# Which activation tables ScalarE loads, and where, in a two-block network (hybrid attention layers and a mixture of experts) on one core

## The chip, the core and the metric

The kernel runs on one core of a Trainium2 chip. The core has five engines with a program of their own each: TensorE (PE in the profile, its weight loads PEld), VectorE (DVE), ScalarE (ACT), GpSimd (POOL) and SyncE (SP), which here only issues DMA transfers. They wait for one another through semaphores. ScalarE evaluates functions such as Exp, Ln and Sigmoid from a table set that has to be loaded before; a load is an instruction of its own, ACT_TABLE_LOAD, on ScalarE's queue. The metric is the device time of one execution in microseconds (us); three executions of the kernel before gave 2309.46, 2310.67 and 2312.57 us.

## The reference, cut to what matters

Everything is float32, one sequence of 256 tokens, width 1024. First come two layers, each a gated delta rule (8 heads) beside a differential attention (8 heads), then one layer of a second block with a mixture of 32 experts, 4 per token.

```
def first_block(x, ...):
    for l in range(2):
        h = rmsnorm(x, norm_w[l])
        proj = h @ w_in[l]
        q_a, k_a, v_a, ab_a, z_a, q_b, k_b, v_b, z_b, gate_a, gate_b = split(proj)
        y_a = gated_delta_branch(q_a, k_a, v_a, ab_a, z_a, ...)
        y_b = diff_attention_branch(q_b, k_b, v_b, z_b, ...)
        merged = sigmoid(gate_a) * (y_a @ w_pa[l]) + sigmoid(gate_b) * (y_b @ w_pb[l])
        x = x + merged @ w_out[l]
    return rmsnorm(x, final_norm_w)

def gated_delta_branch(q, k, v, ab, z, ...):
    qkv = silu(short_conv(concat(q, k, v), conv_w))        # Sigmoid table
    q = l2norm(q); k = l2norm(k)                           # rsqrt as Exp(-0.5 * Ln)
    beta = sigmoid(ab[:2]); g = -exp(a_log) * softplus(ab[2:] + dt_bias)
    o = chunk_gated_delta(forward) + chunk_gated_delta(backward)   # exp of decays
    return rmsnorm(o, norm_w) * silu(z)

def diff_attention_branch(q, k, v, z, ...):
    a = softmax(q0 k0) - lam * softmax(q1 k1)
    return rmsnorm(a @ v, subln_w) * (1 - lambda_init) * silu(z)

def second_block(x, ...):
    h = rmsnorm(x, g_mix); z = h @ w_in
    x = x + concat(pool_mixer(u), dilated_attention(q, k, v)) @ w_out
    x = x + moe(rmsnorm(x, g_ffn), ...)                    # 32 experts, 4 per token
    x = x + (p @ w_ple_proj) * sigmoid(rmsnorm(x, g_ple) @ w_ple_gate)
    return rmsnorm(x, g_final)

def expert_block(xb, e):
    g, u = split(xb @ w_gate_up[e] + b_gate_up[e])
    g = min(g, 7); u = clip(u, -7, 7)
    return ((u + 1) * g * sigmoid(1.702 * g)) @ w_down[e] + b_down[e]
```

## The kernel before

Each engine has its own function, written in the order in which it works; the semaphores between them are set by hand, and nothing reorders the instructions. The loops over layers (l) and heads (n) are unrolled, and the expert loop is a real loop of 32 turns. The one thing that the author of the kernel does not write is most of the table loads: the build puts an ACT_TABLE_LOAD ahead of an activation when the set that it takes for active lacks the function. A call of `preload_act_table_set` puts a load where it stands and names the set that is active from there on. The set "natural_log_exp_and_others" holds both Ln and Exp; the kernel before asks for it at L1041, ahead of the first layer, and at L1319, behind the expert loop. Copy and Square never have a load in front of them.

The stages of a layer, with the names that the text below uses:

- Norm at the layer's start. ScalarE squares and sums the rows of x (L1044), then `ss_rstd` makes 1/sqrt by Ln (L1025) and Exp (L1026); VectorE scales (L1363), TensorE turns the result (`transpose16`, L519). The norm behind the last layer, the norm ahead of the second block and the one ahead of the router use the same `ss_rstd` (their squares are L1020).
- Convolution. TensorE makes the projections (`product`, L527), ScalarE copies them (L1091), VectorE convolves, ScalarE applies Sigmoid to each of 12 units (L1069).
- Segment stage. TensorE makes twelve more products u = 0 to 11 of 16 instructions each (L527). Behind the products u = 0, 1, 2 and 4 it makes two column sums each (`norm_sums`, L578) for the norms of q and k; a sum i waits for ScalarE's square i (`unit_squares`, L1075). Behind the products u = 3, 5, 7 and 9 come two Gram products each (`gram`, L587 and L588), on which VectorE waits (`gram_decay`, L1515). ScalarE, in order: copy of product u (L1106), then for the two sums behind it `unit_rnorms` (Ln at L1081, Exp at L1083) and the square of the unit two further on. The square that TensorE waits for behind product u = 1 thus stands behind the Ln and Exp of the unit two before it. VectorE inverts 16x16 blocks (`invert_base`, L1547 and L1551), four heads at a time, once behind the Gram products of the heads 0 to 3 and once for the heads 4 to 7; head 0 of the head loop cannot get far before the second has ended.
- Head loop, 8 heads. TensorE works at head n and at the rest of head n-1. ScalarE for head n-1: attention_squares (L1148), attention_rstd (Ln L1153, Exp L1154), the z gate in three steps (Exp L1171, Ln L1175, Exp L1179), chunk_rstd (Ln L1142, Exp L1143); for head n the softmax (Exp L1165). The result of L1154 lets VectorE finish head n-1's attention (`attention_y`, L1655), and this frees the bank into which TensorE writes the scores of head n (L663).
- Merge. ScalarE makes the gates' sigmoids from Exp, Ln and Exp (L1219, L1222, L1225), TensorE multiplies (L754, L527), VectorE combines (L1749, L1751).

In the second block there are eight small products for a bias table (L803) behind the last layer, a dilated attention, the router and the expert loop: per turn 64 TensorE instructions for gate and up (L948), 32 for down (L971), one Sigmoid on ScalarE (L1313), and 12.6 MB of weights which SyncE asks for as slots come free. TensorE starts a turn with eight bias products (L939), for which the bias rows, last in the turn's transfers, must have landed.

Of the kernel before, what the change touches and what calls it, by code (L numbers as in the profile page):

```python
# [110 lines left out]
def block_kernel(nc, a, out):  # L111
    ctx = ExitStack()
    with ctx:
# [5 lines left out]
        def s(name):  # L119

            if name not in sems:
                sems[name] = ctx.enter_context(nc.semaphore(name))
            return sems[name]
# [875 lines left out]
        def _(act):  # L999
# [48 lines left out]
            for l in range(DEPTH):  # L1048
# [16 lines left out]
                def sigmoid_unit(u):  # L1065
                    act.wait_ge(s("conv_sb"), l * 12 + u + 1)
                    if u >= 2:
                        act.wait_ge(s("silu_sb"), l * 12 + u - 1)
                    act.activation(sgm[u % 2], conv_o[u % 2], ACT.Sigmoid).then_inc(s("sgm_sb"), 1)  # L1069

                def unit_squares(i):
                    act.wait_ge(s("silu_sb"), l * 12 + NORM_UNITS[i] + 1)
                    if i >= 2:
                        act.wait_ge(s("qk_norm_ps"), l * 8 + i - 1)
                    act.activation(qk_sq[i % 2].rearrange("p (b c) -> p b c", b=2), qkv_unit(NORM_UNITS[i]), ACT.Square).then_inc(s("qk_sq"), 1)  # L1075
# [18 lines left out]
                unit_squares(0)  # L1094
                unit_squares(1)
                sigmoid_unit(11)

                act.wait_ge(s("gcum_cp"), l + 1)
                act.activation(eg[:, :], gcum[:, :], ACT.Exp)
# [198 lines left out]
            def gathered(n):  # L1298
                act.wait_ge(s("gather_ps"), n)
                act.activation(Xs, pb[3][:, :], ACT.Copy).then_inc(s("X_sb"), 1)  # L1300

            def turned(n):
                act.wait_ge(s("XT_ps"), n)
                act.activation(XT, pb[3][:, :].rearrange("p (c h t) -> p c h t", c=4, h=2), ACT.Copy).then_inc(s("XT_sb"), 1)

            gathered(1)
            turned(1)
            act.wait_ge(s("rounds_known"), 1)
# [669 lines left out]
```

## Time and profile before

| | |
|---|---|
| three executions | 2309.46, 2310.67 (median), 2312.57 us |
| profiled execution | 2312.8 us, of which the span from the first to the last instruction is 2311.0 us |
| TensorE busy | 2128.1 us, 92% of the span |
| VectorE busy | 743.6 us, 32% |
| ScalarE busy | 674.7 us, 29% |
| GpSimd busy | 104.8 us, 5% |
| granted TensorE clock, mean | 0.941 of full speed |
| DMA | 551.08 MB, mean 238 GB/s |

How to read it: times are microseconds from the span's start unless marked ns. A timeline row has its start, its busy time, engine, line, operation, output and inputs, how many instructions it merges, and in brackets the idle time of the engine before it and what ended it. TensorE's instructions overlap: a following one starts while the last is in its tail. In the rows by stretch the numbers are the stretch's length, then the busy time (and instructions) of PE, PEld, DVE, ACT and POOL, the granted clock (1.00 is 2.4 GHz, 0.50 is 1.2 GHz), the share of the DMA engines that was busy, and GB/s. In the groups by line, the busy total and the mean in ns of one instruction stand behind the bar, then the idle time ahead of them.

### The profile page before, as it was taken

How to read it: one execution, taken by the hardware profiler on the slowest of the kernel's cores; microseconds unless marked ns; L12 is line 12 of the kernel's file. 1: busy time of each engine (PE TensorE's matmuls, PEld its weight loads, DVE VectorE, ACT ScalarE, POOL GpSimd, SP SyncE). 2: the span in 40 equal slices, each digit the busy share in tenths (PEclk: the TensorE clock that was granted, in tenths of full speed). 3: DMA queues.
4: the chain of work that ended last, by engine and by line, in shares of the span. 5: the costliest groups of instructions: out<-in, count | busy, mean ns of one | idle time of the engine just before them, and what ended most of it. 6: DMA issues, size and time to landing. Idle time of an engine off the chain costs nothing.

```text
span 2311.0 us, 23579 instructions
## 1 busy us (share of the span) xinstructions
PE 2128.1 (92%) x9025; PEld 1095.7 (47%) x9025; DVE 743.6 (32%) x2024; ACT 674.7 (29%) x1210; POOL 104.8 (5%) x84
## 2 busy tenths in 40 slices
PE   4989999998989999999977899999999999999997
PEld 4844777444854677544454433333333333333333
DVE  2657566211565766411131211111111111111112
ACT  2162588421244388721221111111111111111112
POOL 0030111000012121000000000000000000000000
PEclk9999899997999999999877799999999999999998
DMA  5633211343443221345531499999999999999980
GB/s 169 230 117 118 73 37 47 137 145 109 174 154 109 73 74 37 110 145 181 184 155 59 193 427 426 424 428 410 427 415 427 416 428 414 425 428 423 412 358 19
DMA packets 102324, 551.08 MB, mean 238 GB/s; under 512 B 8789, under 2 KB 13041, under 8 KB 77170
## 3 DMA queue, kind: packets, MB, share of 16 engines
q1 hardware_dynamic: 102258, 550.21, 59.4%
q8 instruction: 40, 0.66, 0.1%
q14 instruction: 26, 0.21, 0.0%
HBM read 546.98 MB, written 3.21 MB: 238 GB/s over the span
## 4 chain that ended last, share of the span: by engine, by line
PE 48%; DMA 10%; DVE 4%; ACT 3%; issue 1%; SPq 1%; DVEq 0%
PE bank L948 20%; DMA region<-b_gate_up_dram 10%; PE bank L527 10%; PE bank L971 4%; PE bank L754 2%; PE bank L939 2%; PE bank L921 1%; PE bank L907 1%; PE bank L616 1%; PE bank L519 1%; SPq L389 1%; PE bank L628 0%; PE bank L663 0%; DVE region L1646 0%; PE bank L643 0%
## 5 line engine op out<-in xcount | busy, mean ns | idle before, releaser
L948 PE MATMUL bank<-ring,region 128*64 128x512 f32 x2048 | 474.3, 623 | 0.0
L948 PEld LDWEIGHTS bank<-ring,region 128*64 128x64 f32 x2048 | 150.0, 144 | 326.0 <-issue 326.0
L1889 DVE TENSOR_SCALAR region<-bank 128x512 f32<-128x512 f32 x32 | 22.1, 691 | 755.6 <-PE bank L948 755.6
L527 PE MATMUL bank<-ring,hT 128*128 128x512 f32 x576 | 257.7, 605 | 2.2 <-issue 1.2
L527 PE MATMUL bank<-ring,region 128*128 128x512 f32 x432 | 193.1, 606 | 4.8 <-ACT region L1012 1.8
L527 PEld LDWEIGHTS bank<-ring,hT 128*128 128x128 f32 x576 | 111.4, 195 | 140.3 <-issue 138.8
L527 PE MATMUL bank<-hT,ring 128*128 128x256 f32 x768 | 171.9, 387 | 0.0
L1313 ACT ACTIVATE region<-region 128x512 f32<-128x512 f32 x32 | 20.2, 630 | 519.4 <-DVE region L1889 519.4
L527 PEld LDWEIGHTS bank<-hT,ring 128*128 128x128 f32 x768 | 149.1, 195 | 21.2
L527 PEld LDWEIGHTS bank<-ring,region 128*128 128x128 f32 x432 | 83.7, 195 | 110.6 <-issue 106.8
L971 PE MATMUL bank<-ring,region 128*64 128x512 f32 x512 | 116.9, 597 | 11.3 <-issue 11.3
L616 PE MATMUL bank<-ring,hT 128*128 128x512 f32 x256 | 125.6, 603 | 0.0
L971 PE MATMUL bank<-region 128*64 128x512 f32 x512 | 116.2, 592 | 0.0
L754 PE MATMUL bank<-ring,hT 128*128 128x512 f32 x256 | 111.5, 592 | 0.0
L1317 ACT ACTIVATE region<-bank 128x512 f32<-128x512 f32 x32 | 19.1, 597 | 219.0 <-PE bank L971 219.0
L939 PE MATMUL bank<-region,ones 1*64 1x512 f32 x256 | 38.8, 677 | 46.0 <-DMA region<-b_gate_up_dram 33.9
L1953 POOL TENSOR_TENSOR region<-ring,c_main_sb 128x512 f32<-128x512 f32 x48 | 62.9, 1315 | 353.1 <-PE bank L628 305.2
L1447 DVE SCALAR_TENSOR_TENSOR region<-region,conv_wT 128x256 f32<-128x256 f32 x192 | 78.0, 478 | 0.0
L971 PEld LDWEIGHTS bank<-region 128*64 128x64 f32 x512 | 44.2, 137 | 65.6 <-issue 65.6
L754 PEld LDWEIGHTS bank<-ring,hT 128*128 128x128 f32 x256 | 48.0, 190 | 57.4 <-issue 57.4
L971 PEld LDWEIGHTS bank<-ring,region 128*64 128x64 f32 x512 | 40.4, 136 | 65.7 <-issue 65.7
L921 PE MATMUL bank<-region 64*128 64x512 f32 x264 | 65.8, 615 | 0.7 <-ACT region L1317 0.7
(337 smaller groups left out, 2487.5 us busy)
## 6 DMA issues: line engine op xcount, KB each, us to landing
ring<-w_gate_up_dram SPq DMA_DIRECT2D x128, 2048.0 KB, 11.2
ring<-w_in_dram SPq DMA_DIRECT2D x44, 2048.0 KB, 7.9
ring<-w_down_dram SPq DMA_DIRECT2D x32, 2048.0 KB, 9.9
region<-w_down_dram SPq DMA_DIRECT2D x32, 2048.0 KB, 11.4
ring<-w_out_dram SPq DMA_DIRECT2D x5, 2048.0 KB, 8.1
ring<-rows_scratch SPq DMA_DIRECT2D x4, 2048.0 KB, 9.2
ring<-w_pa_dram SPq DMA_DIRECT2D x4, 2048.0 KB, 8.0
ring<-w_pb_dram SPq DMA_DIRECT2D x4, 2048.0 KB, 8.3
```

The lines of the kernel that those rows point to most:

```text
L389: sp.dma_start(dst, src, **kw).then_inc(s(name), 16)
L519: last = pe.transpose(pb[kp][:, (2 * kk + t) * P:(2 * kk + t + 1) * P], src(t, 2 * kp + kk), ident)
L527: mm = pe.matmul(dst, lhs(k), w(k), start=(k == 0), stop=(k == n_k - 1))
L616: mm = pe.matmul(pb[3][:, :], hT[:, k, t * P:(t + 1) * P], w[:, k, :], start=(k == 0), stop=(k == KC - 1))
L754: mm = pe.matmul(pb[GATE_BANKS[kind][t]][:, :], hT[:, k, t * P:(t + 1) * P], w[:, k, :], start=(k == 0), stop=(k == KC - 1))
L907: mm = pe.matmul(pb[3][hf * 64:(hf + 1) * 64, :], P1[:, t, :], h2[:, t, hf * NB:(hf + 1) * NB], start=(t == 0), stop=(t == 1))
L921: mm = pe.matmul(pb[4 + 2 * t + hf][:, :], CT[hf * 64:(hf + 1) * 64, t, :], ysb[hf * 64:(hf + 1) * 64, :], start=False, stop=False, skip_g ...
L939: pe.matmul(pb[g][hf * 64:(hf + 1) * 64, :], ones[32 * g:32 * g + 1, 0:64], bpad[32 * g:32 * g + 1, hf * NB:(hf + 1) * NB], start=True, st ...
L948: mm = pe.matmul(pb[g][hf * 64:(hf + 1) * 64, :], XT[:, 2 * (j % 2) + kk, j // 2, :], wj[:, kk, c:c + NB], start=False, stop=(j == 3 and k ...
L971: mm = pe.matmul(pb[2][hf * 64:(hf + 1) * 64, :], actT[:, c, j, :], wj[:, c, hf * NB:(hf + 1) * NB], start=(j == 0 and c == 0), stop=(j == ...
L1447: ins = dve.scalar_tensor_tensor(dst, src, w, dst, ALU.mult, ALU.add)
L1953: pool.tensor_tensor(Lv[q].rearrange("p (d t) c -> p d t c", d=2), LT_all[:, n].rearrange("p (d t) c -> p d t c", d=2), lvl[:, q].unsqueez ...
```

## The change

Two lines are added to ScalarE's program. In each layer, behind the last Sigmoid of the convolution, the set with Ln and Exp is asked for by name; ahead of the expert loop, before ScalarE waits for the first gathered tokens, the set with Sigmoid is asked for.

```
                 unit_squares(0)
                 unit_squares(1)
                 sigmoid_unit(11)
+                act.preload_act_table_set("natural_log_exp_and_others")
 
                 act.wait_ge(s("gcum_cp"), l + 1)
                 act.activation(eg[:, :], gcum[:, :], ACT.Exp)
...
                 act.activation(XT, pb[3][:, :].rearrange("p (c h t) -> p c h t", c=4, h=2), ACT.Copy).then_inc(s("XT_sb"), 1)
 
+            act.preload_act_table_set("sigmoid_and_others")
             gathered(1)
             turned(1)
             act.wait_ge(s("rounds_known"), 1)
```

From the first line on, every line number is one higher, and from the second on, two.

ScalarE in the segment stage, kernel before, the copy of product u = 0 and what follows it up to the second square (L1106 is the copy, L1081 and L1083 are Ln and Exp, L1075 is the square):

```order
L1106 ACTIVATE region<-bank 128x512
L1081 ACT_TABLE_LOAD
L1081 ACTIVATE region<-bank,small 128x512
L1083 ACT_TABLE_LOAD
L1083 ACTIVATE region<-region 128x512
L1075 ACTIVATE region<-region 128x512
L1081 ACT_TABLE_LOAD
L1081 ACTIVATE region<-bank,small 128x512
L1083 ACT_TABLE_LOAD
L1083 ACTIVATE region<-region 128x512
L1075 ACTIVATE region<-region 128x512
```

The same place in the changed kernel:

```order
L1107 ACTIVATE region<-bank 128x512
L1081 ACTIVATE region<-bank,small 128x512
L1083 ACTIVATE region<-region 128x512
L1075 ACTIVATE region<-region 128x512
L1081 ACTIVATE region<-bank,small 128x512
L1083 ACTIVATE region<-region 128x512
L1075 ACTIVATE region<-region 128x512
```

The four loads are gone and the order of the rest is kept.

ScalarE in the head loop, kernel before, from the copy ahead of the scores (L1158) to the softmax (L1165) of a head n above 0:

```order
L1158 ACTIVATE region<-bank 128x512
L1153 ACT_TABLE_LOAD
L1153 ACTIVATE small<-small 128x2
L1154 ACT_TABLE_LOAD
L1154 ACTIVATE small<-small 128x2
L1171 ACTIVATE region<-region 128x512
L1119 ACTIVATE region<-bank 128x512
L1134 ACTIVATE region<-bank,eg 128x128 x2
L1175 ACT_TABLE_LOAD
L1175 ACTIVATE region<-region,small 128x512
L1165 ACT_TABLE_LOAD
L1165 ACTIVATE region,small<-bank,small 128x256 x4
```

The same place in the changed kernel:

```order
L1159 ACTIVATE region<-bank 128x512
L1154 ACTIVATE small<-small 128x2
L1155 ACTIVATE small<-small 128x2
L1172 ACTIVATE region<-region 128x512
L1120 ACTIVATE region<-bank 128x512
L1135 ACTIVATE region<-bank,eg 128x128 x2
L1176 ACTIVATE region<-region,small 128x512
L1166 ACTIVATE region,small<-bank,small 128x256 x4
```

Here too four loads are gone; two more go further on in the same head, at L1142 and L1143.

ScalarE around the expert loop in the changed kernel, from the last copy of the router on (L1315 is the Sigmoid in the loop):

```order
L1298 ACTIVATE region<-bank 32x256
L1307 ACT_TABLE_LOAD
L1301 ACTIVATE region<-bank 128x512
L1305 ACTIVATE region<-bank 128x512
L1311 TENSOR_LOAD rounds_i
L1311 ISA x2
L1313 UNCONDITIONAL_BRANCH
L1313 ISA
L1315 ACTIVATE region<-region 128x512
```

In the kernel before the load stood inside the loop, ahead of the Sigmoid; it now stands once, ahead of the loop. In the whole program of the changed kernel nine table loads are left: L1032, L1039 and L1041 at the start, L1069 and L1097 in each layer, L1307, and L1321 behind the expert loop. The other engines' programs are as they were.

## Rows read from the trace of the kernel before

**Rows 1.** Busy time by stretch: up to the expert loop, and the expert loop.

```profile
0.00:1299.00 1299.00, 1188.70 (x4759) 754.45 (x4759) 580.32 (x1684) 538.84 (x1018) 104.75 (x84) 0.93 0.33 119
1299.00:2253.00 954.00, 896.83 (x4160) 321.11 (x4160) 147.23 (x316) 118.55 (x161) 0.00 (x0) 0.97 0.98 415
```

**Rows 2.** Groups of ScalarE by line: table loads, and the loop's Sigmoid.

```profile
L1313 ACT ACT_TABLE_LOAD x32 | 41.1, 1283 | 0.8 <-issue 0.3
L1313 ACT ACTIVATE region<-region 128x512 f32<-128x512 f32 x32 | 20.2, 630 | 519.4 <-DVE region L1889 519.4
...
L1319 ACT ACT_TABLE_LOAD x1 | 1.3, 1283 | 0.0
```

**Rows 3.** Timeline of PE, segment stage of the second layer.

```profile
669.82 7.03 PE L527 MATMUL bank<-ring,hT 128*128 128x512 f32 x16
681.47 1.72 PE L578 MATMUL bank<-region,ones 128*128 128x512 f32 x2 [4.62 <-ACT region L1075]
685.93 2.07 PE L578 MATMUL bank<-region,ones 128*128 128x512 f32 x2 [2.74 <-ACT region L1075]
687.80 9.18 PE L527 MATMUL bank<-ring,hT 128*128 128x512 f32 x16
...
778.03 2.05 PE L628 MATMUL bank<-region 128*128 128x128 f32 x8 [3.78 <-DVE region L1624]
```

**Rows 4.** Timeline of PE, the same place of the first layer.

```profile
151.18 7.84 PE L527 MATMUL bank<-ring,hT 128*128 128x512 f32 x16
```

**Rows 5.** Timeline of ACT, segment stage of the second layer.

```profile
676.97 1.28 ACT L1081 ACT_TABLE_LOAD   x1
678.27 0.69 ACT L1081 ACTIVATE region<-bank,small 128x512 f32<-128x512 f32 x1
...
680.80 0.61 ACT L1075 ACTIVATE region<-region 128x512 f32<-128x512 f32 x1
```

**Rows 6.** Timeline of DVE, segment stage of the second layer.

```profile
706.56 0.69 DVE L1515 TENSOR_TENSOR ring<-ring,bank 128x512 f32<-128x512 f32 x1 [11.07 <-PE bank L588]
```

**Rows 7.** Timeline of PE, end of the first layer's merge.

```profile
493.74 27.63 PE L527 MATMUL bank<-ring,region 128*128 128x512 f32 x64
523.48 2.41 PE L519 MATMUL bank<-c_main_sb,region 128*128 128x128 f32 x16 [2.10 <-DVE region L1751]
526.78 30.14 PE L527 MATMUL bank<-ring,region 128*128 128x512 f32 x64 [0.89 <-issue]
```

**Rows 8.** Busy time by stretch, within the row at 526.78.

```profile
525.00:531.00 6.00, 5.11 (x10) 2.33 (x9) 1.12 (x4) 0.66 (x2) 0.00 (x0) 0.50 0.01 3
```

**Rows 9.** Chain of waits, one head of the second layer (start, us, what).

```profile
841.87 1.28 ACT L1154
...
844.16 1.14 PE bank L663 x8
```

**Rows 10.** Timeline of PE, the instructions ahead of that wait.

```profile
842.95 1.05 PE L628 MATMUL bank<-region 128*128 128x128 f32 x8
```

**Rows 11.** Waits of PE up to 1300 (total, times, longest).

```profile
PE bank L663 <- DVE region L1655: 1.5, 10, 0.2
```

**Rows 12.** Timeline of ACT, norm at the second layer's start.

```profile
558.84 1.28 ACT L1025 ACT_TABLE_LOAD   x1
```

**Rows 13.** Timeline of PE, the three places behind such norms.

```profile
563.61 3.65 PE L519 MATMUL bank<-c_main_sb,region 128*128 128x128 f32 x16 [6.70 <-DVE region L1363]
...
1092.89 12.09 PE L803 MATMUL bank<-region,rel 33*128 33x512 f32 x16 [0.78 <-DVE x L1767]
1106.67 3.68 PE L519 MATMUL bank<-c_main_sb,region 128*128 128x128 f32 x16 [1.70 <-DVE region L1363]
...
1267.26 3.67 PE L519 MATMUL bank<-c_main_sb,region 128*128 128x128 f32 x16 [7.71 <-DVE region L1365]
```

**Rows 14.** Chain of waits, two turns of the expert loop.

```profile
1686.78 16.60 PE bank L948 x64
...
1717.75 13.91 PE bank L948 x64
```

More of the change, by code:

```diff
@@ L1096, in _ @@
                 sigmoid_unit(11)
+                act.preload_act_table_set("natural_log_exp_and_others")
                 act.wait_ge(s("gcum_cp"), l + 1)
@@ L1304, in turned @@
                 act.activation(XT, pb[3][:, :].rearrange("p (c h t) -> p c h t", c=4, h=2), ACT.Copy).then_inc(s("XT_sb"), 1)
+            act.preload_act_table_set("sigmoid_and_others")
             gathered(1)
```

## The prediction

> **What bounds the kernel now.** I read the busy time by stretch first [rows 1]. TensorE is busy for 1188.7 of the first 1299 us and for 897 of the 954 us of the expert loop; in the loop the DMA engines are busy for 0.98 of the time at 415 GB/s, so the loop goes by the transfers, with TensorE close behind. ScalarE is busy for 539 us in the first part and 119 us in the loop: nowhere the bound as a whole. So what its table loads cost can't be had from their sum. It has to be looked for where TensorE stands still and the wait leads back through ScalarE, and in the views of the waits there are few such places: the segment stage of each layer, one wait in each head, and the norms between the stages.
>
> **The loads that go.** The groups of ScalarE by line list 194 loads in 22 groups, from 32 at L1313 to one at L1319, each 1.283 us [rows 2]. Nine are left, so 185 go, 237 us of ScalarE's time. A load takes 1.30 us out of a chain: 676.97 to 678.27 [rows 5], that is 1.28 and a gap of 0.02. The load that now stands behind the last Sigmoid of the convolution is the one that stood one line further on; it costs nothing new.
>
> The Trainium skill (ScalarE: Activation LUTs, section on what ACT_TABLE_LOAD costs) adds a drain of 1380 ns to the 1283 ns of a load, 2.66 us for a switch. The trace doesn't agree: the activation starts 1.30 us behind the load's start, as said. By the page each load below would count twice, and the norms alone would bring some 5 us more; I go by the row.
>
> **Segment stage.** Here is most of the gain. In the second layer TensorE has ended product u = 1 at 681.47 - 4.62 = 676.85, waits 4.62 us for the square of L1075, makes one column sum, waits 2.74 us for the next square, and starts product u = 2 at 687.80 [rows 3]. On ScalarE two loads lie ahead of the first of these squares and four ahead of the second, from 676.97 on without a gap [rows 5]. What releases that chain at 676.97 is VectorE's work on the decays and stays. So the first sum comes 2.60 us earlier, at 678.87, and the second 5.20 us earlier, at 680.73. The two waits shrink to about 2.0 and 1.0 us. TensorE's 16 instructions take 7.03 us at full clock [rows 3], so about 0.86 for the two of a sum: product u = 2 starts at 681.6, 6.2 us earlier.
>
> The clock comes on top. The product at 687.80 took 9.18 us instead of 7.03: 2.15 us lost because the granted clock had fallen in the wait to the lower of its two levels, 1.2 of 2.4 GHz. In the first layer the same product took 7.84 us, 0.81 lost [rows 4]. If the clock now stays up in the shorter waits, the second layer gains 6.2 + 2.15 = 8.4 and the first 6.2 + 0.8 = 7.0, together 15.4 us. If it falls, each layer loses again about what the wait at the end of the merge costs: 2.10 us of waiting, then a product of 64 instructions in 30.14 instead of 27.63 us, 2.5 us lost at a clock of 0.50 [rows 7, 8]. Then the two gain 15.4 - 5.0 = 10.4. The wait of 2.10 us is just as long as the one that stays here, so the fall is likelier; I take 12 us, 6 for each layer. Ends: nothing (a rival below) and 15.4.
>
> Does it last? What follows is driven by TensorE: VectorE waited 11.07 us for the Gram product at 706.56 [rows 6], and it then works almost without a pause until it releases head 0's next step at 778.03, for which TensorE had waited 3.78 us [rows 3]. VectorE's chain begins with that Gram product, so it moves with TensorE, and so does the start of the head loop. ScalarE has slack behind it: the squares for the later sums are ready before their product ends already now. The weights' transfers run at 119 GB/s against 415 in the loop [rows 1], so they keep up.
>
> **Head loop.** A head takes some 20.6 us, and TensorE has hardly a gap in it. The chain passes through the loads of L1153 and L1154 and VectorE's L1655 to the scores at 844.16 [rows 9]. But the instructions ahead of the scores start at 842.95 and are busy for 1.05 us, up to 844.00 [rows 10]: of the 2.60 us that leave this chain TensorE can use 0.15, which is the wait that the profile lists, 1.5 us in ten heads [rows 11]. There are 14 such heads: 14 x 0.15 = 2.1 us. Ends: nothing, and 14 x 0.32 = 4.5 us if the scores could start as tightly as other products do (0.16 us ahead of their predecessor's end). The other four loads of a head lie under TensorE's work: the softmax comes 2 us earlier, but VectorE, which needs it, is at that time still busy with the keys, and the step behind it waits for VectorE. ScalarE falls from nearly full in a head to some three fifths; nobody there waits for it any more.
>
> **Norms.** `ss_rstd` has two loads in four of its six calls, 2.60 us each call [rows 12]. At the second layer's start and ahead of the router TensorE waits for the norm alone, 6.70 and 7.71 us [rows 13]: 2.6 us each, 5.2. The clock is down at both places, and waits of 4.1 and 5.1 us leave it down. The two calls behind the last layer follow one another, 5.2 us in all, but TensorE makes the bias table's products beside them: those run from 1092.89 for 12.09 us, to 1104.98, and the next work started at 1106.67 [rows 13]. So 1.7 us can be had, and 3.5 are hidden. Together 6.9 us; ends 5.2 and 8.
>
> **Merge, gates, expert loop.** The merge's 16 loads lie beside products of 27 us, for which VectorE waits anyway: nothing. In the expert loop the load ran right behind the turn's last copy, with 0.8 us of idle time before all 32, and the Sigmoid then waited 519.4 us for VectorE [rows 2]: removing 41.1 us of loads there brings nothing. The load added ahead of the loop lies in ScalarE's wait for the first gathered tokens, which is longer than 10 us: nothing; 1.3 us if that cover were gone. Behind it only the copies of the first tokens are queued. The loop as a whole starts earlier by the whole gain, since its transfers start when TensorE frees the first slot; the first expert's weights have landed well before.
>
> **Sum.** 12 + 2.1 + 6.9 = 21.0 us. The profiled execution took 2312.8 us, so 2291.8; it stood 2.1 us above the median of 2310.67, which gives 2289.7 us.
>
> **Rivals.**
> The clock stays up. The waits of 2.0 and 1.0 us leave the granted clock at its upper level in both layers, and the heads give their upper end: 15.4 + 4.5 + 6.9 = 26.8 us, 2283.9 us. For it: at the waits of now the clock was lost for only 0.81 us in one of the layers. Against: the fall behind a wait of 2.10 us [rows 7].
>
> The segment stage gives its gain back. Product u = 2 starts earlier, but VectorE or the decays become the bound ahead of the head loop, so that only heads and norms are left: 9.0 us, 2301.7 us. For it: TensorE already waits 3.78 us for VectorE there. Against: VectorE's own idle 11.07 us, which say that it is TensorE that feeds it.
>
> Nothing happens. Either the loads weren't in anyone's way, or the expert loop's transfers, the real bound, don't start earlier: 2310.7 us. Against: the transfers of the loop wait for slots that TensorE frees. A rule of the Trainium skill would have it so as well: by the page ScalarE activation tables: per-element evaluation and per-set limits, section on table sets in the compiler and the runtime, the loads are placed by the longest run that one set serves, and then Ln beside Exp would have shared a set already. The trace of before doesn't agree: each Ln and each Exp of L1081 and L1083 has its own load.
>
> Slower. The expert loop sits at the edge between transfers and TensorE's clock: a turn whose gate and up products meet the lower clock has them in 16.60 instead of 13.91 us, and takes 1717.75 - 1686.78 = 31.0 us [rows 14] against a mean of 954 / 32 = 29.8 [rows 1]. If the earlier start put all turns into that state, they would cost 32 x 1.2 = 38 us: 2289.7 + 38 = 2328 us. It decides from 18 such turns on. Against: a turn that long lets the transfers get ahead, the wait at its start goes, and with it the reason for the fall.
>
> **Chances.** The forecast 0.63 (its own range 2286 to 2294), the clock staying up 0.15, the gain given back 0.13, nothing 0.04, slower 0.05. The range, 2281 to 2301 us, holds the first two and half of the third. A change of less than 0.2%, 4.6 us, can't be told from none here: faster by more 0.92, the same 0.03, slower 0.05.
>
> **What would show it.** The profile after should have 9 table loads and ScalarE busy for about 437 us. In both layers the two waits of L578 should be near 2.0 and 1.0 us, VectorE's first wait for a Gram product some 2 us longer than 11.07 (it is fed sooner by ScalarE than by TensorE), and the wait of 3.78 us ahead of head 0 unchanged. The wait for L1655 ahead of the scores should be gone, with heads of 20.4 us. The norm waits should read 4.1 and 5.1 us, and the one behind the bias table none. The expert loop should take 954 us as before. It is wrong if the head loop starts no earlier against the layer's start, if another engine's wait grows there by what L578 loses, or if the loop's length moves by more than 3 us.

## The result, and the profile after

The changed kernel takes 2274.82 us (median; 2273.50 to 2275.65), beside 2310.07 us of the kernel before on the same chip: a ratio of 0.9844 with a 95% interval of 0.9831 to 0.9856, or 35 us less. The forecast was 2289.7 us, 21 us less, and 2281 to 2301 as a range. The direction was right, and the time lies outside the range: two fifths of the gain weren't foreseen.

The profiled execution took 2274.37 us, its span is 2272.6 us, the mean granted clock 0.956 (before 0.941). The busy time of the engines, from the profile page:

```profile
PE 2108.8 (93%) x9025; PEld 1086.3 (48%) x9025; DVE 739.3 (33%) x2024; ACT 435.7 (19%) x1025; POOL 104.8 (5%) x84
```

ScalarE is busy for 435.7 us, where 437 was expected. TensorE is busy for 19.3 us less than before, although its 9025 instructions are the same ones. What differs is the granted clock, and for the clock the forecast had some 3 us at most (2.15 and 0.8 in the two segment stages): the first sign of what it left out. Busy time by stretch, up to the expert loop and in the loop (columns as in [rows 1]):

```profile
0.00:1261.70 1261.70, 1169.29 (x4757) 745.13 (x4757) 576.12 (x1684) 340.88 (x865) 104.77 (x84) 0.95 0.34 122
1261.70:2216.20 954.50, 898.62 (x4160) 321.64 (x4160) 147.15 (x316) 77.50 (x129) 0.00 (x0) 0.96 0.98 414
```

The loop is as long as it was, 954.5 against 954.0 us; the 37.3 us that are gone by its start were gained ahead of it. Timeline of TensorE in the segment stage of the second layer, beside [rows 3]:

```profile
665.21 1.12 PE L578 MATMUL bank<-region,ones 128*128 128x512 f32 x2 [1.92 <-ACT region L1075]
666.97 1.13 PE L578 MATMUL bank<-region,ones 128*128 128x512 f32 x2 [0.63 <-ACT region L1075]
667.93 7.03 PE L527 MATMUL bank<-ring,hT 128*128 128x512 f32 x16
...
756.01 2.05 PE L628 MATMUL bank<-region 128*128 128x128 f32 x8 [3.77 <-DVE region L1626]
```

The waits of 4.62 and 2.74 us are 1.92 and 0.63 now, and the clock stayed up: the product takes its full-clock 7.03 us, where it took 9.18. VectorE still waits for the first Gram product, 11.37 against 11.07 us [rows 6], and the wait of 3.77 us ahead of head 0 is what it was, so the gain goes on into the head loop:

```profile
684.54 0.69 DVE L1517 TENSOR_TENSOR ring<-ring,bank 128x512 f32<-128x512 f32 x1 [11.37 <-PE bank L588]
```

The chain of waits in one head of the second layer (start, us, what), beside [rows 9], no longer passes through ScalarE:

```profile
818.27 0.89 PE bank L628 x8
819.16 1.07 PE bank L663 x8
```

And TensorE at the first layer's end, at the second layer's start, behind the last layer and ahead of the router, beside [rows 7, 13]:

```profile
515.14 1.97 PE L519 MATMUL bank<-c_main_sb,region 128*128 128x128 f32 x16 [2.10 <-DVE region L1753]
518.00 27.70 PE L527 MATMUL bank<-ring,region 128*128 128x512 f32 x64 [0.90 <-ACT region L1012]
549.84 3.65 PE L519 MATMUL bank<-c_main_sb,region 128*128 128x128 f32 x16 [4.14 <-DVE region L1365]
...
1077.44 3.67 PE L519 MATMUL bank<-c_main_sb,region 128*128 128x128 f32 x16
...
1232.19 3.39 PE L519 MATMUL bank<-c_main_sb,region 128*128 128x128 f32 x16 [5.15 <-DVE region L1367]
1236.47 5.10 PE L527 MATMUL bank<-region,hT 128*128 128x32 f32 x32 [0.89 <-ACT hT L1012]
```

The norms' waits fell by 2.56 us each, 6.70 to 4.14 and 7.71 to 5.15, and the 1.70 us behind the bias table are gone. But look at what stands next to them. At the first layer's end TensorE waits the same 2.10 us as before, and the product of 64 instructions takes 27.70 us where it took 30.14 [rows 7]. In the router, 32 instructions take 5.10 us. The kernel before has them in 7.01:

```profile
1271.83 7.01 PE L527 MATMUL bank<-region,hT 128*128 128x32 f32 x32 [0.89 <-issue]
```

No load went from the first of these places. In the router none stood between these instructions either, but the wait ahead of them had lost two; experiments 2 and 5 have the same instructions behind a wait that is not shortened.

**The ledger.** Since TensorE's instructions are the same in both kernels, the start of each can be compared one by one. Of the stages' lengths I took the mean over four profiled executions on each side (the kernel before with e2, e5 and e6 of the experiments below, the kernel after with e1, e7 and e8: they differ from these two only in the loop's loads, or by one or two loads ahead of the first norm):

| | gained, us | forecast |
|---|---|---|
| segment stage, first and second layer | 7.3 and 7.9 | 12 for both |
| heads | 3.1 in 14 heads | 2.1 |
| norms | 2.56, 2.1 and 2.56 | 6.9 |
| granted clock, where no load left | 9.4 | none |
| start (first transfers), expert loop, end | 1.2 early, then 2.4 lost | 0 |
| sum | 33.7 | 21.0 |

The 9.4 us are 1.8 in the first layer's last products, 1.2 in the two first heads, 1.7 in the second layer's last products, 1.4 in the second block's z products, 1.0 between those and the router and 2.3 from the router to the gathering. The row of the start and the loop scatters by as much between executions of one kernel. So do two parts of the 9.4: the first heads (88 instructions behind TensorE's wait of 3.78 us took 16.1 to 19.6 us in the executions before, 16.1 to 18.9 after) and the first layer's last products, where one of the four executions before, e6, lost no more than the kernel after.

### The profile page after: what moved, and what is told of

Its sections match the earlier page's. It is cut to its first block, busy times and chain, and to the rows that moved or that the text cites. A ratio compares the mean times of both kernels' runs of the same rounds, so it can differ in the third digit from the quotient of the medians.

```text
span 2272.6 us, 23394 instructions
## 1 busy us (share of the span) xinstructions
PE 2108.8 (93%) x9025; PEld 1086.3 (48%) x9025; DVE 739.3 (33%) x2024; ACT 435.7 (19%) x1025; POOL 104.8 (5%) x84
## 4 chain that ended last, share of the span: by engine, by line
PE 51%; DMA 10%; DVE 4%; ACT 1%; issue 1%; SPq 1%; DVEq 0%
PE bank L948 21%; PE bank L527 10%; DMA region<-b_gate_up_dram 10%; PE bank L971 5%; PE bank L754 2%; PE bank L939 2%; PE bank L616 1%; PE bank L921 1%; PE bank L907 1%; PE bank L628 1%; SPq L389 1%; PE bank L639 1%; PE bank L519 1%; PE bank L803 1%; DVE region L1648 0%
## 5 line engine op out<-in xcount | busy, mean ns | idle before, releaser
L527 PE MATMUL bank<-ring,hT 128*128 128x512 f32 x576 | 251.1, 592 | 2.2 <-issue 1.2
L527 PE MATMUL bank<-ring,region 128*128 128x512 f32 x432 | 189.4, 597 | 4.8 <-ACT region L1012 3.6
L527 PEld LDWEIGHTS bank<-ring,hT 128*128 128x128 f32 x576 | 108.7, 190 | 135.1 <-issue 133.6
L527 PE MATMUL bank<-hT,ring 128*128 128x256 f32 x768 | 171.5, 386 | 0.0
L527 PEld LDWEIGHTS bank<-hT,ring 128*128 128x128 f32 x768 | 148.7, 194 | 21.0
L527 PEld LDWEIGHTS bank<-ring,region 128*128 128x128 f32 x432 | 82.3, 192 | 107.9 <-issue 101.9
L1315 ACT ACTIVATE region<-region 128x512 f32<-128x512 f32 x32 | 20.2, 630 | 561.8 <-DVE region L1891 561.8
L616 PE MATMUL bank<-ring,hT 128*128 128x512 f32 x256 | 125.0, 601 | 0.0
L971 PE MATMUL bank<-region 128*64 128x512 f32 x512 | 116.2, 592 | 0.0
L754 PE MATMUL bank<-ring,hT 128*128 128x512 f32 x256 | 111.5, 592 | 0.0
L907 PE MATMUL bank<-region 128*64 128x512 f32 x264 | 63.7, 604 | 0.0
```

Of the source, the lines that this page charges most:

```text
L527: mm = pe.matmul(dst, lhs(k), w(k), start=(k == 0), stop=(k == n_k - 1))
L616: mm = pe.matmul(pb[3][:, :], hT[:, k, t * P:(t + 1) * P], w[:, k, :], start=(k == 0), stop=(k == KC - 1))
L754: mm = pe.matmul(pb[GATE_BANKS[kind][t]][:, :], hT[:, k, t * P:(t + 1) * P], w[:, k, :], start=(k == 0), stop=(k == KC - 1))
L907: mm = pe.matmul(pb[3][hf * 64:(hf + 1) * 64, :], P1[:, t, :], h2[:, t, hf * NB:(hf + 1) * NB], start=(t == 0), stop=(t == 1))
L971: mm = pe.matmul(pb[2][hf * 64:(hf + 1) * 64, :], actT[:, c, j, :], wj[:, c, hf * NB:(hf + 1) * NB], start=(j == 0 and c == 0), stop=(j == ...
```

## Experiments

**1. Which of the two calls.** Kernel after without the call ahead of the loop, and kernel before with that call alone.

```
-            act.preload_act_table_set("sigmoid_and_others")     # e1: from after
+            act.preload_act_table_set("sigmoid_and_others")     # e2: into before
             gathered(1)
```

> The change without the second call: Ln and Exp share a set in the layers, the Sigmoid's load stays inside the expert loop (32 loads). Theory (the loop's loads lie in ScalarE's wait and cost nothing): the same as the changed kernel, 2274.8 us, within 1.5 us. Rival (the loop's loads are worth something, for example 0.3 us a turn, which would explain part of the 14 us that the forecast missed): 2284 us or more, and a longer expert loop than 954 us.

Measured: 2276.62 us (2274.18 to 2279.37), ratio to the kernel before 0.9851 [0.9835, 0.9866].

> The second call alone: 32 loads leave the expert loop, all of the layers' loads stay. Theory: the same as before, 2310.1 us within 1.5 us, the expert loop at 954 us. Rival (loop loads cost): 2300 us or less.

Measured: 2310.43 us (2305.08 to 2317.12), ratio 1.0006 [0.9994, 1.0018]. The gain comes from the call in the layer: e1 is far from its rival's 2284 us, though 1.8 us above the changed kernel, where the theory allowed 1.5. The 32 loads of the loop stood in an idle time of 519 us [rows 2] and were worth nothing that these runs show, as forecast. Over the profiles of this document the loop took 953.5 to 957.7 us with them and 952.0 to 956.6 without, so a us would not be seen.

**2. The segment stage alone, and all but it.** From the kernel after: the loads return behind product u = 9 by asking for another set there, or the call is made only there.

```
                 for u in range(12):
                     act.wait_ge(s("seg_ps"), l * 12 + u + 1)
+                    if u == 9:      # e3, with the call of after kept
+                        act.preload_act_table_set("exp_and_others")
+                    if u == 9:      # e4, in place of the call of after
+                        act.preload_act_table_set("natural_log_exp_and_others")
```

> The set with Ln and Exp serves only from the convolution's end to segment product 9; behind that another set with Exp alone is asked for, and the loads of heads, merge and norms come back as before. Theory (the segment stage's waits and their clock are 7.1 and 8.2 us by the comparison of the two traces): 2310.1 - 15.4 = 2294.7 us, the waits of L578 at 2.0 and 1.0 us, the clock up behind them in both layers. Second theory (an earlier start also moves later stages against the falls of the clock): up to 10 us less than that, 2285 us. Rival (the forecast's 12 us): 2298 us.

Measured: 2285.80 us (2283.65 to 2289.55), ratio 0.9897 [0.9877, 0.9917]: 24.9 us less than before, where the second theory had put it.

> The loads of the segment stage stay (16 Ln and 16 Exp in the two layers), all others leave. Theory by waits alone: heads 3.1 us and norms 7 us by the comparison of the traces, 2300 us. Second theory (the rest of the gain, 23 us of span, belongs to these stages and to the clock behind them): 2287 us. Between the two would show that part of the clock's gain hangs on where the segment stage ends, not on the loads that left.

Measured: 2295.00 us (2292.61 to 2295.43), ratio 0.9931 [0.9916, 0.9947]: 15.7 us less, between the two theories' 2300 and 2287 us. The two gains make 40.6 us, more than the 34 to 35 of both together, so part of each is one that either of them brings. In e3 the segment stages are 15.7 us shorter than in the profiled execution before. The other 9 lie elsewhere, where e3 has the same loads as the kernel before. The plainest place is the router (timeline of TensorE, e3), behind the unshortened wait of 7.71 us for the norm:

```profile
1245.76 3.68 PE L519 MATMUL bank<-c_main_sb,region 128*128 128x128 f32 x16 [7.71 <-DVE region L1369]
1250.33 4.49 PE L527 MATMUL bank<-region,hT 128*128 128x32 f32 x32 [0.90 <-issue]
```

The same wait, the same 32 instructions, and 4.49 in place of 7.01 us. The length of the wait just ahead does not decide what the clock costs.

**3. The program as a whole later.** If it were the absolute time at which a wait falls, a delay far ahead would shift all of it. One or two loads more (1.3 us each) ahead of the first norm, in the kernel before (e5, e6) and after (e7, e8).

```
                 in_layer.fence()
+                if l == 0:
+                    for name in NAMES:      # one name, or two
+                        act.preload_act_table_set(name)
                 ss_rstd(in_layer)
```

> The kernel before with one table load more (1.3 us) ahead of the first norm, on the path of everything: all that follows is 1.3 us later and otherwise as it was. Theory A (the gain that the waits don't explain comes from where in time the waits fall against the clock's own rhythm, and that is fixed to the program's start): the time moves by something other than 1.3 us, by 3 us or more either way, so not within 2310.5 to 2313.5. Theory B (the clock falls by chance from execution to execution, and its mean loss depends on the waits alone): 2312.0 us, within 1.5.

Measured: 2312.40 us, ratio 1.0013 [1.0004, 1.0022].

> The kernel before with two table loads more (2.6 us) ahead of the first norm. Theory A: off the straight line by 3 us or more here or in the run with one load. Theory B: 2313.3 us within 1.5.

Measured: 2311.45 us, ratio 1.0010 [1.0001, 1.0019].

> The changed kernel with one table load more (1.3 us) ahead of the first norm. Theory A: off 2276.5 us by 3 us or more, up to 2285, since a favourable place is lost. Theory B: 2276.5 us within 1.5.

Measured: 2276.62 us, ratio 0.9851 [0.9836, 0.9867].

> The changed kernel with two table loads more (2.6 us) ahead of the first norm. Theory A: off 2277.8 us by 3 us or more here or in the run with one load. Theory B: 2277.8 us within 1.5.

Measured: 2277.74 us, ratio 0.9869 [0.9854, 0.9884]. The medians moved by 2.4 and 1.5 us in the kernel before and by 1.8 and 2.9 us in the kernel after (beside the 2274.82 us measured on another chip), for 1.3 and 2.6 us added. None is off by the 3 us that theory A asked for; e6 is 1.9 us below theory B's figure, which allowed 1.5. In the profiles the early stages scatter: the 64 instructions of [rows 7] took 27.70 us in e6, the kernel before with two more loads:

```profile
529.16 27.70 PE L527 MATMUL bank<-ring,region 128*128 128x512 f32 x64 [0.89 <-ACT region L1012]
```

But late stages came out alike however late the program had started: from the router to the gathering 21.62 us in e5 and e6 beside 21.63 before, 19.69 and 19.74 us in e7 and e8 beside 19.72 after.

From this I formed a second theory: what the clock costs at a wait is set by how much work lies between it and the last fall of the clock. By this theory a fall takes up the shift that the program brings along, behind it the program stands against the falls of the clock as it does in every execution of the same kernel, and a change of the work in between, as the one studied here, moves all later falls. One run already at hand fits only in part: e1, whose program is the kernel after's up to the loop, took 18.93 us in that stage and not 19.7.

**4. More work, no other wait.** The theory's test: the kernel before with r more product instructions (0.86 us each; the trace counts each as two) at the start of the second layer's merge. Their result is overwritten, and no load or wait is changed.

```
+                if l == 1:
+                    w = w_wait(l, 16)
+                    for _ in range(r):      # 1, 2, 3
+                        pe.matmul(pb[GATE_BANKS[0][0]][:, :], hT[:, 0, 0:P], w[:, 0, :], start=True, stop=True)
                 gate_part(0, 0, 0, range(0, 4))
```

> The kernel before with one more product instruction (about 0.86 us of TensorE's work, its result overwritten) at the start of the second layer's merge; no table load is changed. Theory A (where a wait falls against the clock's rhythm decides what the clock costs there, and that goes by the amount of work since the clock's last fall): the stages behind it change their lengths although nothing in them is changed: the output product at the second layer's end (28.49 us to the bias products before, against 28.48 in the changed kernel; 4.15 us ahead of it against 2.86), the z products of the second block (62.85 against 60.87) or the stage from the router to the gathering (21.62 against 18.9 to 19.7), by 0.5 us or more in at least one; the time is off 2310.9 by a us or more in one of the three kernels with more work. Theory B (the clock's loss hangs on the length of the waits alone): all later stages keep their lengths to 0.1 us, and the time is 2310.0 + 0.9 = 2310.9 us.

Measured: 2307.92 us (2303.50 to 2310.12), ratio 0.9987 [0.9977, 0.9997].

> As the kernel with one more product instruction there, with two (about 1.7 us). [...] Theory B: later stages as before, 2310.0 + 1.7 = 2311.7 us.

Measured: 2309.86 us, ratio 0.9999 [0.9990, 1.0008].

> As the kernel with one more product instruction there, with three (about 2.6 us). Theory A: again other lengths of the later stages than with one and with two, time anywhere from 2308 to 2315 us, not on one line with the two others. Theory B: later stages as before, 2310.0 + 2.6 = 2312.6 us.

Measured: 2310.40 us, ratio 1.0005 [0.9992, 1.0017]. The kernel before ran at 2310.75 us beside them. Behind the merge TensorE turns 16 tiles and makes the output product. In the kernel before (first row) the turn was in part at the lower level of the clock; with two more instructions (second row, e10) it was at the upper one, as in the kernel after:

```profile
1060.26 3.25 PE L519 MATMUL bank<-c_main_sb,region 128*128 128x128 f32 x16 [2.11 <-DVE region L1751]
```

```profile
1059.42 1.97 PE L519 MATMUL bank<-c_main_sb,region 128*128 128x128 f32 x16 [2.11 <-DVE region L1755]
1062.28 27.70 PE L527 MATMUL bank<-ring,region 128*128 128x512 f32 x64 [0.90 <-ACT region L1016]
```

The wait is 2.11 us in both. One caution: executions of one kernel still differ here. Ahead of the edit they come in groups, told apart by the stage of head 0 of the second layer (from the 3.8 us wait on). In the group of 19.5 us the turn and the product together (L519 to the bias table) took 32.63, 32.65, 32.62 and 32.65 us without added work (before, e2, e6 and e12 below), and 31.35 with two instructions more. In the group of 17.1 us they took 34.22 us twice without (e5, e14), 32.67 with one (e9) and 31.35 with three (e11). Within these two groups each addition shortened what follows, by 1.3 to 2.9 us for 0.9 to 2.6 us of work. But e13 below, the kernel before's program up to here, stood in neither group (19.9 us) and took 31.35 us with nothing added, so this value alone does not show an effect of the added work. The stage from the router on was 21.62 us in all three, as without added work.

**5. The same in the second block,** where 4.7 of the 9.4 us had been gained: r more such instructions ahead of the last z product.

```
+                for _ in range(r if u == 7 else 0):      # 1, 2, 3
+                    pe.matmul(pb[7][:, :], hT[:, 0, P:2 * P], slot_w(slot)[:, 0, :], start=True, stop=True)
                 product(pb[4 + u % 4][:, :], ...
```

> The kernel before with one more product instruction (0.86 us at full clock) ahead of the last z product of the second block; no load is changed. Theory A (position against the clock's falls, set by the work since the last one): one or more of the three stages behind it change by 0.5 us or more: to the first turn for the router (before: 38.36 us with the norm's loads), the router's stage up to the gathering (21.62), and the mixer's (54.67). In the kernel with the segment loads alone removed they read 37.20, 19.12 and 54.64 with the same instructions as before. Theory B: these three stay to 0.1 us, and the time is 2310.5 + 0.9 us.

Measured: 2306.56 us (2303.55 to 2312.81), ratio 0.9984 [0.9974, 0.9995].

> As the one with one more product instruction ahead of the last z product, with two (1.7 us). Theory A: one of the three with more work reads 19.0 to 20.0 us in the stage from the router to the gathering in place of 21.62, so that added work is given back. Theory B: 21.62 in all three, the time 2310.5 + 1.7 us.

Measured: 2308.67 us, ratio 0.9992 [0.9983, 1.0002].

> As the two before, with three (2.6 us). Theory A: the stages behind it differ from those with one and with two by half a us or more, so the time is not on one line with them. Theory B: stages as before, the time 2310.5 + 2.6 us.

Measured: 2308.57 us, ratio 0.9988 [0.9977, 0.9999]. The kernel before: 2309.34 us beside them. Timeline of TensorE, e12, where the kernel before has 7.01 us:

```profile
1268.98 4.19 PE L527 MATMUL bank<-region,hT 128*128 128x32 f32 x32 [0.89 <-issue]
```

The kernel does 0.86 us more work, and its median is 2.8 us lower (by the interval 1.2 to 6.0). From the first z product to the loop it takes 186.39 us with one more, 185.64 with two and 186.44 with three, and 187.62 without. By the rival these would be 188.5, 189.3 and 190.2. So the profiled executions gain 1.2 to 2.0 us by the loop's start. The stage of 19.0 to 20.0 us that was expected of one of the three came with three more (19.40); it is 0.6 us off the one with one more and 0.4 off the one with two, where 0.5 was asked for. The granted clock shows it in the stretch of the 32 instructions (the kernel before, then e12, by stretch):

```profile
1272.00:1279.00 7.00, 6.84 (x32) 6.70 (x32) 0.55 (x3) 0.00 (x0) 0.00 (x0) 0.50 0.58 228
```

```profile
1269.00:1273.20 4.20, 4.17 (x32) 4.04 (x32) 0.64 (x2) 0.00 (x0) 0.00 (x0) 0.87 0.94 372
```

The table puts the executions side by side, in us: from the last turn of the second layer (L519) to the bias table, from the mixer (L826) to the router's turn (2.56 us added where the norm's loads are gone), and from the router (L527) to the gathering (L907). No wait in these stages lost a load but the norm's.

| kernel | L519 to bias table | L826 to router's turn | router to L907 |
|---|---|---|---|
| before, e2, e6 | 32.62 to 32.65 | 93.04 to 93.05 | 21.62 to 21.63 |
| e5 | 34.22 | 93.04 | 21.62 |
| after, e7, e8 | 31.34 to 31.35 | 91.71 to 91.77 | 19.69 to 19.74 |
| e1 | 31.35 | 93.03 | 18.93 |
| e3 | 31.35 | 91.85 | 19.12 |
| e4 | 31.35 | 93.18 | 18.68 |
| e9, e10, e11 | 32.67, 31.35, 31.35 | 93.04 | 21.62 |
| e12, e13, e14 | 32.65, 31.35, 34.22 (ahead of the edit) | 93.04, 92.00, 91.56 | 18.81, 18.99, 19.40 |

The last column settles for the second block that the clock's cost is no property of the waits: seven executions of the kernel before, plain, without the loop's loads, or with loads added at the start or work in the second layer's merge, read 21.62 or 21.63 us, and three with more work just ahead read 18.8 to 19.4. It does not settle the second theory. In e3 the loads and the work are the kernel before's from the second layer's product u = 9 on, the clock fell several times in between, and the stage still reads 19.12; and e1 differs from the kernel after by 0.8 us at the same program. Both stood in the group of e13 at head 0 of the second layer. So what happened some hundreds of us earlier can reach this stage.

**6. The wait that was left.** In both kernels ScalarE's copy of product u = 0, with the Ln, Exp and squares behind it, stands behind four decay exponentials (L1087), which wait for VectorE. The kernel after with these four behind the squares:

```
-                for n in range(4):
-                    decay_exp(n)
                 for u in range(12):
...
                                 unit_squares(i + 2)
+                    if u == 0:
+                        for n in range(4):
+                            decay_exp(n)
                     if u == 1:
```

> The changed kernel with ScalarE's first four decay exponentials of a layer (L1087, which wait for VectorE) moved from ahead of the copy of product u = 0 to behind it and the two squares that follow. The squares for the sums behind product u = 1 are then ready before that product ends. Main theory (these waits were ScalarE's queue behind VectorE's decays): the waits of about 2.0 and 1.0 us in each layer go, the products start 3 us earlier in each layer, and the time is 2274.8 - 6 = 2268.8 us, with up to 3 us more or less by where the clock falls in the later stages. Rival (the Gram products and with them the head loop hang on VectorE's decays, which now come later, or the wait only moves to the sums behind product u = 2): 2273 to 2276 us.

Measured: 2264.51 us (2258.00 to 2265.87), ratio to the kernel before 0.9797 [0.9783, 0.9812], some 10 us faster than the changed kernel and 4.3 us below the expected 2268.8, for which 3 us were allowed. Timeline of TensorE in the second layer: the waits for L1075 are gone.

```profile
647.84 1.02 PE L578 MATMUL bank<-region,ones 128*128 128x512 f32 x2
648.69 7.03 PE L527 MATMUL bank<-ring,hT 128*128 128x512 f32 x16
655.56 1.88 PE L578 MATMUL bank<-region,ones 128*128 128x512 f32 x4
657.28 7.03 PE L527 MATMUL bank<-ring,hT 128*128 128x512 f32 x16
```

The two segment stages became 3.1 and 3.3 us shorter, as expected. Most of the other 4 us came in head 0 of the first layer, which took 18.90 us after and 15.54 here, behind a wait of 3.78 us in both; e1 had 16.12 there with the program of the kernel after. It is the clock again, by stretch (the kernel after, then this one):

```profile
238.00:242.00 4.00, 4.00 (x18) 3.70 (x18) 1.96 (x7) 1.93 (x8) 0.00 (x0) 0.50 0.00 0
```

```profile
234.00:238.00 4.00, 4.00 (x26) 3.04 (x26) 3.58 (x13) 1.93 (x8) 0.00 (x0) 0.99 0.00 0
```

It is the fastest version found.

## Why the prediction was wrong

**What held.** Nothing is won in the merge and the expert loop, and nothing of the segment stage's gain is given back: the rival that VectorE becomes the bound there is out by the 11.37 us of its wait (though the forecast had it grow to some 13 us). The waits of L578 came out at 1.92 and 0.63 us for a forecast of 2.0 and 1.0, the norms at 7.2 us for 6.9. The Trainium skill (ScalarE: Activation LUTs, What ACT_TABLE_LOAD costs) has 2.66 us for a switch, by which estimate two loads cost 5.3 us at a norm. The trace doesn't agree: the two norm waits fell by 2.56 us, so 1.28 us a load was the right price. The rival with nothing happening falls as well.

**Two terms too small.** The segment stage gained 15.2 us, the forecast's upper end (15.4), for which it had 12. The step that failed is "The wait of 2.10 us is just as long as the one that stays here, so the fall is likelier". Behind waits of 1.92 and 0.63 us the clock stayed up in both layers, in all executions with these loads gone. The heads gave 0.22 us each and not 0.15, between the forecast and its end of 0.32: the scores can start a little ahead of their predecessor's end. Together these make some 4 us, and with them the forecast would have been 2285.5, inside the range and near the rival in which the clock stays up.

**One term missing, and the larger.** This is the step that took the time out of the range: the forecast put the clock's effect on all stages without a removed load at nothing, and gave no row for it. It took the clock's loss as a property of each wait, so a place with no load removed had nothing to gain, and where loads went it said "The clock is down at both places, and waits of 4.1 and 5.1 us leave it down". For the turn itself that holds (3.65 us as before [rows 13]). But how long it stays down behind it changes: 5.10 and not 7.01 us in the router, and 2.3 us in all from there to the gathering. The same happened in five other stages, 9.4 us in all by the means. Experiments 2 and 5 show it without any change of the waits there; experiment 4 points the same way, with e13's execution against it. They also show that this share doesn't belong to the loads as such: one superfluous product instruction made the router's stage 2.8 us shorter. Which falls get cheaper by a change could not have been read from one profile of the kernel before; that it differs at equal waits could: behind 2.10 us in the first layer the product took 30.14 us and not 27.63 [rows 7], behind 2.11 us in the second it was the turn that took longer, and the product was at full clock. This would have asked for a term with both signs and a wider range. Where the 9.4 us were gained I can say stage by stage, but not by a rule, and that they are a gain here and no loss was not foreseeable from anything shown.

**Left open.** The theory formed in experiment 3 was borne out where work was added just ahead of a stage. It fails to account for e1 and e3, so the cause of the repeats, and of the changes, is known only this far: not the length of the wait, but something that earlier stages hand on. At which position a fall is dear or cheap I haven't worked out. Nor are the medians of e9 to e11 explained to the us: they hold executions of several groups in shares that the profiles don't show.

## What to carry to other kernels

Load removals are worth what the waits behind ScalarE's chain lose, at 1.28 us a load, and nothing where the engine idles; so find the waits of TensorE that lead back to ScalarE, and leave the busy total alone. Where waits of some microseconds break TensorE's work, give any change a further term for the clock, of either sign, at the places that it does not touch (here 9 of 35 us), and compare the stages of the two traces by instruction before crediting an edit. When a wait shrinks but stays, look at what stands ahead in the queue of the engine it leads to: moving four instructions brought another 10 us.

## What the runs showed of the hardware

VectorE's 32 decay instructions of a layer (L1508) took 15.05 us in the kernel after and 6.36 in the fastest version (timelines of VectorE and GpSimd, second layer, the kernel after; then the fastest):

```profile
653.60 15.05 DVE L1508 TENSOR_SCALAR ring<-ring,gcum 128x128 f32<-128x128 f32 x32
655.28 1.36 POOL L1946 TENSOR_TENSOR ring<-ring,c_main_sb 128x512 f32<-128x512 f32 x1 [285.86 <-ACT ring L1087]
656.72 1.40 POOL L1948 TENSOR_TENSOR ring<-ring 128x512 f32<-128x512 f32 x1
```

```profile
646.03 6.36 DVE L1509 TENSOR_SCALAR ring<-ring,gcum 128x128 f32<-128x128 f32 x32
652.33 2.38 POOL L1947 TENSOR_TENSOR ring<-ring,c_main_sb 128x512 f32<-128x512 f32 x1 [290.25 <-ACT ring L1087]
```

In the first GpSimd starts as soon as ScalarE has the first exponential, and works on without a pause beside VectorE. In the second it starts when VectorE is done. One line's answer on all 64 of these instructions gives shortest, median and longest in ns, for the kernel after and for the fastest:

```profile
L1508 DVE TENSOR_SCALAR ring<-ring,gcum x64: 270/280/1370, 131.6 to 668.4; 128x128 f32<-128x128 f32 x64
```

```profile
L1509 DVE TENSOR_SCALAR ring<-ring,gcum x64: 278/282/284, 130.7 to 652.1; 128x128 f32<-128x128 f32 x64
```

The longest, 1370 ns, is as long as one of GpSimd's instructions (1.36 us). In the kernel after 16 of the 64 took 1356 to 1370 ns, each began less than 0.2 us into one of the 16 instructions that GpSimd ran meanwhile and ended 0.1 us behind it; eight times the 1.08 us between long and short make the 8.7 us by which 15.05 exceeds 6.36. The Trainium skill (SBUF — State Buffer, SBUF: two separate sides) says that the two engines' shared port pair is a lock held for a whole instruction, and that the other one blocks, if VectorE's instruction is in a 2-port mode or has two inputs in SBUF. The trace agrees with the blocking, 1370 against 280 ns; in which mode these instructions ran it does not show. So the wait that the forecast put down to "VectorE's work on the decays" was in good part GpSimd's. That this is what held the decays was seen beside the edit, not tried by itself.

The other surprise is how well one stage repeats, and on what little it turns: after delays of 1.3 and 2.6 us at the start the stage from the router on took 21.62 us each time, and one instruction of 0.86 us put in 110 us ahead of it made it 18.81. In e3, with the kernel before's program for the last 500 us, it was 19.12; what hands such a change on no run here shows.
